# Folding the modulation weights on VectorE instead of multiplying them on TensorE, in a two-block transformer kernel

## The chip, the cores and the metric

The kernel runs on one core of one Trainium2 chip. The core has a matrix engine (TensorE, PE in the profile; its weight loads are PEld), a vector engine (VectorE, DVE), an activation engine (ScalarE, ACT), GpSimd (POOL) and a queue that issues most transfers (SyncE, SP). SBUF is the working memory, PSUM holds what TensorE writes. The metric is the time of one execution on the device in microseconds (us); lower is better.

## What is computed

Two blocks of two layers each on 256 tokens of width 1024, all in f32. The first block is a diffusion-style one: a vector `c` (for the latent tokens) and a vector `c_ctx` (for 256 context tokens) give, per layer, six modulation vectors of length 1024 each:

```python
for l in range(2):
    mod   = silu(c)     @ w_ada[l] + b_ada[l]          # w_ada[l]: 1024 x 6144
    mod_c = silu(c_ctx) @ w_ada[l] + b_ada[l]
    sh1, sc1, g1, sh2, sc2, g2 = split(mod, 6)         # the same for mod_c: csh1, ...
    h  = rms_norm(x,  norm1_g[l]) * (1 + sc1)  + sh1
    hc = rms_norm(xc, norm1_g[l]) * (1 + csc1) + csh1
    y, yc = mixer_sublayer(h, hc, ...)                 # qkv, Fourier mix, two attentions, gates, w_out
    x = x + g1 * y
    h = rms_norm(x, norm2_g[l]) * (1 + sc2) + sh2
    x = x + g2 * expert_choice_ffn(h, ...)             # 16 experts, each takes 32 tokens
    if l == 0:                                         # the same for the context tokens
        xc = xc + cg1 * yc
        xc = xc + cg2 * expert_choice_ffn(modulated rms_norm(xc), ...)
```

In layer 1 only the latent tokens go on, so `c_ctx` counts there for sh1 and sc1 alone. The second block (three kinds of attention and a cross attention to a memory, two layers) is not touched.

## The kernel before

All large weights stream through `ring`, four slots of 2 MB in SBUF. `slab_plan` (L53) writes down the order of all slabs; SP issues them in that order (L597 to L603), and slab i waits until slab i-4 has been used. TensorE tells that in order, with `last_release` (L717: a drain of the engine, then an increment of `slab_used`).

A layer of the first block has a **mixer** and an **experts** stage. In the mixer TensorE does three slabs of qkv products (`qkv_group`, four token tiles t each), three slabs of gates (`gate_group`, b = 0 to 2, four column groups j each), the attention (`pairs_pe`), one slab of branch products, three slabs of gates (b = 3 to 5) and one more of branches. VectorE copies odd qkv tiles out of PSUM, takes the sums of squares of the q and k heads (L2123 and L2124), waits for ScalarE's root of them (`rstd`, L1975), scales the heads and rotates them (L2133 to L2138, L2064 to L2069), then serves the attention (`pairs_dve`) and multiplies and adds the gated branches (L2162 to L2170). TensorE transposes the rotated heads in `turn_heads` (L843), the first of them behind gate group (1, 2).

The experts stage starts with two w_out slabs (L973), the second norm, the router logits (L991) and the choice of tokens, a chain of small steps on VectorE that ends with `slots` (L2262) and `select` (L2269). TensorE then gathers the chosen tokens (L1024), and goes through 16 experts: four slabs of gate and up weights (L1159), transposes (L1181) and two slabs of down weights (L1194). Between its waits it is kept busy with throwaway matmuls (`keep_warm`, L722).

The 24 slabs of `w_ada` (12 a layer, 512 columns each; slab n is called ada n) are handled in three steps. `ada_product` (L697) multiplies a slab by both vectors on TensorE, 32 matmuls of which each has a 128x32 operand `CT` (two columns of it are the two vectors, the rest is zero) and 128 columns of weights; four of them write to four groups of 32 partitions. ScalarE copies the result (`ada_row`, L1544), TensorE transposes it (`ada_turn`, L711), and ScalarE adds the bias into `MODT` (`ada_column`, L1551). Ada 0 to 3 are done at the very start. Ada 4 to 17 are spread over the mixer of layer 0, a product behind every second group and its transpose behind the next. Ada 18 to 21 lie at the start of the experts of layer 0 (18 behind the first tile's transpose, 19 and 20 between the gathers, 21 ahead of expert 0, its transpose behind expert 0's gate and up products and ahead of `scaled_rows`, L1048). Ada 22 and 23 lie at the start of the experts of layer 1. Their slabs stand in the plan at the same places: ahead of the slab that follows them in the mixer, and behind the two w_out slabs for 18 to 23.

Of the kernel before, what the change touches and what calls it, by code (L numbers as in the profile page):

```python
# [19 lines left out]
ALU = mybir.AluOpType  # L20
# [3 lines left out]
P = 128  # L24
# [10 lines left out]
RING = 4  # L35
# [10 lines left out]
ADA_LAST = 18  # L46
# [5 lines left out]
def slab_plan():  # L52

    plan = []
    for l in range(DEPTH):
        mixer = [("qkv", s) for s in range(3)] + [("gate", s) for s in range(3)] + [("branch", 0)]
        mixer += [("gate", 3 + s) for s in range(3)] + [("branch", 1)]
        for n, (kind, s) in enumerate(mixer):
# [14 lines left out]
    for l in range(DEPTH):  # L73
# [9 lines left out]
            {(0, 0): 4, (0, 1): 5, (1, 0): 0, (1, 1): 1}]  # L83

# [12 lines left out]
def shared_signals():  # L97
# [28 lines left out]
    ada_done=12, ada_mm=12, ada_row=12, ada_turned=12, mod=3, ld_dft=32, qk_turned=8, qkt=8, rope=4,  # L126
# [37 lines left out]
def build(nc, a, out, ctx):  # L164
# [40 lines left out]
    ct = sb("ct", KC * 32)  # L205
    modt = sb("modt", DEPTH * 96)
# [78 lines left out]
    CT = ct[:, :].rearrange("p (k n) -> p k n", k=KC)  # L285
    WR = wr[:, :].rearrange("p (l k e) -> p l k e", l=DEPTH, k=KC)
# [61 lines left out]
    slab_used = sem("slab_used")  # L348

# [321 lines left out]
    def _(pe):  # L671
# [9 lines left out]

        def ada_product(n, b=6, held=False):
# [6 lines left out]
            if n == 0:  # L689
                pe.wait_ge(*at("ct", 1))  # L690
            elif n >= ADA_LAST:
                pe.wait_ge(*at(f"ada_done@{l}", s))
            else:
                pe.wait_ge(*(at(f"ada_row@{l}", m) if m else at("ada_row@0", 12)))
            for k in range(KC):
                for j in range(4):
                    mm = pe.matmul(ps[b][32 * j:32 * j + 32, 0:P], CT[:, k, :],  # L697
                                   w[:, k, paired(j) if 6 <= s < 10 else slice(j * P, j * P + P)],
                                   start=(k == 0), stop=(k == KC - 1))
# [146 lines left out]
        def mixer(l):  # L846
# [37 lines left out]
            for s in (1, 2):  # L884
                for t in range(4):
                    qkv_group(l, s, t)
                    if l == 0:
                        step = 2 * (s - 1) + t // 2
                        if t % 2 == 0:
                            if s == 2:  # L890
                                ada_product(4 + t // 2)
                            fourier_tokens(0, step)
                        else:
                            if s == 2:
                                ada_turn(4 + t // 2)
# [6 lines left out]
            for b in range(3):  # L902
                for j in range(4):
                    gate_group(l, b, j, tokens)
                    if l == 0:
                        ada = 6 + 2 * b + j // 2
                        if j % 2 == 0:
                            ada_product(ada)
                        else:
# [1862 lines left out]
```

## Time and profile before

| what | us |
|---|---|
| median of 3 runs | 2285.1 |
| lowest and highest | 2284.4, 2285.84 |
| profiled execution, whole | 2280.98 |
| profiled execution, span of the core | 2279.1 |

| stage | us of the span | TensorE | transfers |
|---|---|---|---|
| start and mixer, layer 0 | 0 to 458 | nearly always busy | about half the time |
| experts, layer 0 | 458 to 1042 | busy | at their rate (415 to 424 GB/s) from about 600 on |
| mixer, layer 1 | 1042 to 1267 | busy | about a third |
| experts, layer 1 | 1267 to 1810 | waits for transfers | at their rate from 1328 on |
| second block | 1810 to 2279 | busy | about a quarter |

A row of the timeline gives start and duration in us, engine, line, operation, output and inputs by their names, shapes, and in brackets the idle time ahead of it with what ended it. "issue" stands for idle time that no other engine's work explains. A row can merge several instructions (x64). An f32 matmul is two instructions in these counts. Differences of two starts are the time from one piece of work to the next, which is less than a duration where instructions overlap.

### The profile page before, as it was taken

The page shows a single profiled execution, that of the slowest core. Times are in us where ns is not written, and L with a number is a line of the kernel's source. Part 1 is how long each engine was busy: PE and PEld are TensorE (multiplying, and loading weights), DVE is VectorE, ACT ScalarE, POOL GpSimd, SP SyncE. Part 2 cuts the span into 40 slices and gives each one's busy share as a digit, 9 for nine tenths or more (in the row PEclk, how much of TensorE's full clock was granted, in tenths as well). Part 3 has the DMA queues.
Part 4 walks back from the last instruction along what each step waited for, and adds up shares of the span by engine and source line. Part 5 has one row for each costly group of instructions (what it writes and reads, how often), then busy time and mean ns, then how long its engine had stood idle before and what let it go on. Part 6 is the DMA issues. An engine that isn't in the chain of part 4 may idle for free.

```text
span 2279.1 us, 31723 instructions
## 1 busy us (share of the span) xinstructions
PE 1986.8 (87%) x13681; PEld 1093.5 (48%) x13681; DVE 623.2 (27%) x1483; ACT 435.3 (19%) x1095; POOL 26.9 (1%) x52
## 2 busy tenths in 40 slices
PE   7999999999988898889999975667776699999997
PEld 4445554456434444334768641233432347564765
DVE  2012640135112221223351321201101235333533
ACT  2122621013111111002161110100000122222222
POOL 3000000000000000000000000000000000000000
PEclk9999999999999999999999997889989999999999
DMA  9544244227899999994314589999999933233320
GB/s 290 185 160 173 75 142 171 94 74 272 349 424 421 423 422 422 420 419 170 129 57 185 217 353 424 423 416 415 418 415 419 364 111 111 87 135 111 111 83 19
DMA packets 133832, 576.03 MB, mean 253 GB/s; under 512 B 7448, under 2 KB 16128, under 8 KB 92736
## 3 DMA queue, kind: packets, MB, share of 16 engines
q1 hardware_dynamic: 129312, 556.82, 61.8%
q0 software_dynamic: 3872, 17.00, 2.2%
q8 instruction: 110, 1.80, 0.3%
q10 hardware_dynamic: 512, 0.19, 0.0%
q14 instruction: 26, 0.21, 0.0%
HBM read 572.93 MB, written 1.05 MB: 252 GB/s over the span
## 4 chain that ended last, share of the span: by engine, by line
PE 53%; DMA 19%; issue 10%; PEld 8%; DVE 5%; PEldq 2%; ACT 2%; SPq 0%; POOL 0%; DVEq 0%; POOLq 0%
DMA ring<-w_up_e 14%; PE ps L788 8%; PE ps L1159 6%; PE ps L1250 5%; PE ps L973 4%; PE ps L1258 3%; PEld ps L1194 3%; PE ps L804 2%; PE ps L1392 2%; PE ps L777 2%; PEldq L717 2%; DMA ring<-w_xkv 2%; DMA ring<-w_down_e 2%; PE ps L1226 1%; PE ps L1229 1%
## 5 line engine op out<-in xcount | busy, mean ns | idle before, releaser
L1159 PE MATMUL ps<-ring,reg_bc 128*32 128x512 f32 x2960 | 382.4, 653 | 125.9 <-DMA ring<-w_up_e 118.1
L1159 PEld LDWEIGHTS ps<-ring,reg_bc 128*32 128x32 f32 x2960 | 91.9, 115 | 393.7 <-DMA ring<-w_up_e 199.8
L788 PE MATMUL ps<-reg_a,ring 128*128 128x512 f32 (+1 forms) x768 | 253.9, 488 | 5.5 <-issue 4.4
L788 PEld LDWEIGHTS ps<-reg_a,ring 128*128 128x128 f32 x768 | 143.5, 190 | 104.6 <-issue 92.7
L2352 DVE TENSOR_TENSOR xall<-xall,ps 128x512 f32<-128x512 f32 x48 | 32.8, 687 | 446.0 <-PE ps L1125 446.0
L1250 PE MATMUL ps<-ring,reg_a 128*128 128x512 f32 (+2 forms) x448 | 142.7, 474 | 2.6 <-issue 2.3
L1760 ACT ACTIVATE reg_bc<-ps 128x512 f32<-128x512 f32 x48 | 28.7, 597 | 562.4 <-PE ps L1159 562.4
L2395 DVE TENSOR_TENSOR reg_a<-ps,reg_e 32x256 f32<-32x256 f32 x192 | 80.7, 420 | 199.8 <-PE ps L1194 197.4
L1194 PE MATMUL ps<-ring,reg_bc 128*32 128x256 f32 x2048 | 117.8, 380 | 16.2 <-issue 14.7
L777 PE MATMUL ps<-ring,reg_a 128*128 128x512 f32 (+1 forms) x288 | 112.8, 546 | 1.9 <-issue 1.5
L1250 PEld LDWEIGHTS ps<-ring,reg_a 128*128 128x128 f32 x448 | 74.0, 190 | 65.1 <-issue 63.7
L1194 PEld LDWEIGHTS ps<-ring,reg_bc 128*32 128x32 f32 x2048 | 70.3, 110 | 54.7 <-issue 21.1
L1194 PE MATMUL ps<-ring,reg_e 128*32 128x256 f32 x1024 | 67.2, 406 | 31.4 <-issue 17.6
L1258 PE MATMUL ps<-reg_a,ring 128*128 128x256 f32 x384 | 88.9, 390 | 6.1 <-ACT reg_d L1798 5.0
L804 PE MATMUL ps<-reg_d,ring 128*128 128x512 f32 (+1 forms) x256 | 84.2, 488 | 1.7 <-issue 0.8
L973 PE MATMUL ps<-ring,reg_bc 128*128 128x512 f32 x192 | 84.2, 594 | 0.6 <-issue 0.5
L1258 PEld LDWEIGHTS ps<-reg_a,ring 128*128 128x128 f32 x384 | 74.0, 196 | 17.0 <-issue 7.0
L777 PEld LDWEIGHTS ps<-ring,reg_a 128*128 128x128 f32 x288 | 54.2, 190 | 56.2 <-issue 54.5
L804 PEld LDWEIGHTS ps<-reg_d,ring 128*128 128x128 f32 x256 | 48.1, 190 | 35.6 <-issue 30.4
L1568 ACT ACTIVATE reg_e<-ps 128x512 f32<-128x512 f32 (+1 forms) x48 | 23.6, 491 | 207.9 <-PE ps L788 207.8
L1194 PEld LDWEIGHTS ps<-ring,reg_e 128*32 128x32 f32 x1024 | 34.5, 116 | 57.1 <-issue 29.2
L1705 ACT ACTIVATE reg_bc<-ps,modt,scl 128x128 f32<-128x128 f32 x96 | 36.2, 458 | 129.2 <-PE ps L1024 129.2
(356 smaller groups left out, 2161.5 us busy)
## 6 DMA issues: line engine op xcount, KB each, us to landing
ring<-w_down_e SPq DMA_DIRECT2D x64, 2048.0 KB, 14.9
ring<-w_gate_e SPq DMA_DIRECT2D x123, 1024.0 KB, 10.6
ring<-w_up_e SPq DMA_DIRECT2D x123, 1024.0 KB, 13.6
ring<-w_in SPq DMA_DIRECT2D x34, 2048.0 KB, 8.1
ring<-w_ada SPq DMA_DIRECT2D x24, 2048.0 KB, 8.2
ring<-w_out SPq DMA_DIRECT2D x8, 2048.0 KB, 7.9
ring<-w_xkv SPq DMA_DIRECT2D x8, 1024.0 KB, 14.1
ring<-w_br_global SPq DMA_DIRECT2D x4, 1024.0 KB, 6.4
```

The costliest lines, as they stand in the source:

```text
L717: pe.drain().then_inc(slab_used, 1)
L777: mm = pe.matmul(ps[t][:, c0:COL], HT[:, k, t * P:t * P + P], w[:, k, c0:COL], start=(k == 0), stop=(k == KC - 1))
L788: mm = pe.matmul(ps[j][:, 0:n], w[:, k, j * P:(j + 1) * P], HT[:, k, 0:n], start=(k == 0), stop=(k == KC - 1))
L804: mm = pe.matmul(ps[n % 4][:, 0:tokens], w[:, k, j * P:(j + 1) * P], OT[:, k, 0:tokens], start=(k == k0), stop=(k == k1 - 1))
L973: mm = pe.matmul(ps[b][:, :], MT[:, k, t * P:t * P + P], w[:, k, :], start=(k == 0), stop=(k == KC - 1))
L1159: mm = pe.matmul(ps[s][32 * j:32 * j + 32, :], XGT[l][:, e // 4, s, 2 * q + k, e % 4 * CAP:(e % 4 + 1) * CAP], w[j // 2][:, k, (j % 2) * C ...
L1194: mm = pe.matmul(ps[4 + s][32 * j:32 * j + 32, 0:SEQ], HE[l][:, s, k, q * CAP:(q + 1) * CAP], w[:, k, j * SEQ:(j + 1) * SEQ], start=(q == ...
L1250: fill(name, lambda b: [pe.matmul(ps[b][:, 0:c1 - c0], src[:, k, t * P:t * P + P], w[:, k, c0:c1], start=(k == 0), stop=(k == KC - 1)) for ...
L1258: fill(name, lambda b: [pe.matmul(ps[b][:, 0:SEQ], w[:, k, c * P:(c + 1) * P], src[:, k, :], start=(k == 0), stop=(k == KC - 1)) for k in ...
L1392: yield pe.matmul(ps[b][:, :], OT2[:, k, t * P:t * P + P], w[:, k, :], start=(q == 0), stop=(q == KC - 1))
L1705: ins = act.activation(XGT[l][:, g, s, k, :], ps[6 + h][:, kk * P:(kk + 1) * P], ACT.Identity, scale=SCL[:, l, 1, k, s:s + 1], bias=MODT[: ...
L2395: ins = dve.tensor_tensor(OE[l][r:r + CAP, e // 4 % 2, s, j * SEQ:(j + 1) * SEQ], ps[4 + s][CAP * j:CAP * (j + 1), 0:SEQ], GB[CAP * j:CAP ...
```

## The change

The slabs ada 4 to 23 no longer go through TensorE whole. VectorE folds each of them (`fold`): for each of the 8 rows k that a partition holds it multiplies the 512 weights by that row's element of the vector, and adds it to a running sum. For ada 4 to 15 that is done for both vectors, in 16 instructions (2 of `tensor_scalar`, 14 of `scalar_tensor_tensor`). From ada 16 on only the latent tokens' vector is used; the even and the odd rows have a sum each, in 8 instructions (2 and 6). An instruction waits for the one before the last (semaphore `fold`), which writes the sum that it reads. TensorE (`ada_sum`) adds the two sums over the partitions: 8 matmuls, with `pick` (ones in one column, zeros in the others) as the 128x32 operand. A slab is given back by VectorE (`ada_folded`), so SP waits for VectorE at 20 places of its order.

The places move too. Ada 4 to 19 are all in the mixer of layer 0, ada 20 to 23 in the mixer of layer 1, by the table `ADA_STEPS` on TensorE and ScalarE, and each slab stands in the plan behind the mixer's slab. Nothing of them is left in the experts stages. On VectorE the folds stand at fixed places: 4 to 7 ahead of its four qkv copies, 8 and 9 between the sums of squares and the wait for the root, 10 to 12 ahead of the attention, 13 to 19 (in layer 1: 20 to 23) between the two halves of the branch merges.

```diff
@@ slab_plan
-            if l == 0 and 2 <= n < 9:
-                plan += [("ada",) + divmod(ada, 12) for ada in (2 * n, 2 * n + 1)]
-            plan.append((kind, l, s))
+            early = [("ada",) + divmod(ada, 12) for ada in ADA_BEHIND[l].get(n, ())]
+            plan += [(kind, l, s)] + early
         plan += [("out", l, s) for s in range(2)]
-        plan += [("ada", 1, s) for s in ((6, 7, 8, 9), (10, 11))[l]]
@@ sync
-                sp.wait_ge(slab_used, i - RING + 1)
+                sp.wait_ge(*slab_freed(i - RING))
@@ tensor
+        def ada_sum(n, b=6):
+            l, s = divmod(n, 12)
+            pe.wait_ge(*at(f"ada_folded@{l}", s + 1 - (0 if l else ADA_FOLDED)))
+            pe.wait_ge(*(at(f"ada_row@{l}", s) if s else at("ada_row@0", 12)))
+            for v in range(2):
+                chosen = 0 if n >= ADA_ALONE else v
+                for j in range(4):
+                    mm = pe.matmul(ps[b][32 * j:32 * j + 32, 0:P], pick[:, 32 * chosen:32 * chosen + 32],
+                                   folded(n)[:, v, paired(j) if 6 <= s < 10 else slice(j * P, j * P + P)],
+                                   start=(v == 0), stop=(v == 1))
+            mm.then_inc(sem(f"ada_mm@{l}"), 1)
@@ tensor, experts
             turn_tile(0)
-            if l == 0:
-                pe.wait_ge(*at("rexp@0", 1))
-            first = (18, 22)[l]
-            ada_product(first, 2)
+            keep_warm((6, 2)[l], 12)
             logits(0)
@@ vector
+        def fold(n):
+            ...
+            slab_wait(dve, i)
+            if n >= ADA_FOLDED + 2:
+                m = n - 2
+                dve.wait_ge(*(at(f"ada_mm@{m // 12}", m % 12 + 1)))
+            turns = [(k, v, k) for k in range(KC) for v in range(2)] if n < ADA_ALONE else [(k // 2, k % 2, k) for k in range(KC)]
+            for turn, v, k in turns:
+                c = CT[:, k, 0:1] if n >= ADA_ALONE else CT[:, k, v:v + 1]
+                if turn == 0:
+                    ins = dve.tensor_scalar(sums[:, v, :], w[:, k, :], c, None, ALU.mult)
+                else:
+                    dve.wait_ge(*at("fold", folds[0] - 1))
+                    ins = dve.scalar_tensor_tensor(sums[:, v, :], w[:, k, :], c, sums[:, v, :], ALU.mult, ALU.add)
+                ...
@@ vector, mixer
             dve.sem_inc(sem(f"qn@{l}_total"), 1)
+            if l == 0:
+                fold(8)
+                fold(9)
             rstd(f"qn@{l}", 40, HD)
+            if l == 0:
+                for n in (10, 11, 12):
+                    fold(n)
             pairs_dve(dve, link, f"at@{l}", pairs_block1(l))
             for half in range(2):
+                if half:
+                    for n in (range(13, 20), range(20, 24))[l]:
+                        fold(n)
+                    modulation(l, 1)
```

VectorE in the mixer of layer 0, before: from the last sums of squares to the scaling of the heads (`st` holds the sums and roots, `norm_rs` is ScalarE's root).

```order
L2123 TENSOR_TENSOR reg_d<-reg_bc 128x640 [waits dve_step]
L2124 TENSOR_REDUCE st<-reg_d 128x10 [waits dve_step]
L1973 TENSOR_SCALAR st<-st 128x40 [waits dve_step]
L1975 TENSOR_TENSOR st<-st 128x40 [waits norm_rs,dve_step]
L1976 TENSOR_TENSOR st<-st 128x40 [waits dve_step]
```

The same place after the change (`ada_mm` is TensorE's sum of an earlier slab, `ring` the weights, `ct` the vectors).

```order
L2151 TENSOR_TENSOR reg_d<-reg_bc 128x640 [waits dve_step]
L2152 TENSOR_REDUCE st<-reg_d 128x10 [waits dve_step]
L2060 TENSOR_SCALAR reg_d<-ring,ct 128x512 [waits dve_step,ada_mm,slab_landed0]
L2060 TENSOR_SCALAR reg_d<-ring,ct 128x512
L2063 SCALAR_TENSOR_TENSOR reg_d<-ring,ct,reg_d 128x512 [waits fold] x14
L2060 TENSOR_SCALAR reg_e<-ring,ct 128x512 [waits ada_mm,slab_landed1]
L2060 TENSOR_SCALAR reg_e<-ring,ct 128x512
L2063 SCALAR_TENSOR_TENSOR reg_e<-ring,ct,reg_e 128x512 [waits fold] x14
L1973 TENSOR_SCALAR st<-st 128x40
L1975 TENSOR_TENSOR st<-st 128x40 [waits norm_rs,dve_step]
```

Thirty-two instructions on slabs ada 8 and 9 now stand ahead of the wait for the root.

TensorE at the end of the choice of tokens in layer 0, before (L1024 gathers, L697 are products on a slab, L1006 turns the slots, L1159 is expert 0).

```order
L1024 MATMUL ps<-tmp,reg_d 128x128 [waits sel_first]
L1024 MATMUL ps<-tmp,reg_d 128x128 x7
L697 MATMUL ps<-ring,ct 32x128 [waits ada_done,slab_landed1]
L697 MATMUL ps<-ring,ct 32x128 x31
L1006 MATMUL ps<-ident,reg_e 128x16 [waits slots]
...
L1024 MATMUL ps<-tmp,reg_d 128x128 [waits xgt,sel_first]
L1024 MATMUL ps<-tmp,reg_d 128x128 x7
L697 MATMUL ps<-ring,ct 32x128 [waits ada_done,slab_landed2]
L697 MATMUL ps<-ring,ct 32x128 x31
L1159 MATMUL ps<-ring,reg_bc 32x512 [waits xgt,slab_landed3]
```

The same place after the change.

```order
L1055 MATMUL ps<-tmp,reg_d 128x128 [waits sel_first]
L1055 MATMUL ps<-tmp,reg_d 128x128 x7
L1037 MATMUL ps<-ident,reg_e 128x16 [waits slots]
L1037 MATMUL ps<-ident,reg_e 128x16
L1055 MATMUL ps<-tmp,reg_d 128x128 [waits xgt,sel_first]
L1055 MATMUL ps<-tmp,reg_d 128x128 x7
...
L1178 MATMUL ps<-ring,reg_bc 32x512 [waits xgt,slab_landed1]
```

The products on ada 20 and 21 are gone from between the gather and the slots, and from ahead of expert 0.

## Rows read from the trace of the kernel before

**Rows 1.** The page's second part: transfers in 40 equal slices, tenths busy.

```profile
DMA  9544244227899999994314589999999933233320
```

**Rows 2.** Timeline of TensorE in mixer 0: first and last product, and what follows.

```profile
103.18 1.96 PE L697 MATMUL ps<-ring,ct 128*32 128x128 f32 x64
105.42 1.96 PE L820 MATMUL ps<-tmp,reg_bc 128*128 128x512 f32 x4 [0.29 <-issue]
...
392.64 1.95 PE L697 MATMUL ps<-ring,ct 128*32 128x128 f32 x64
394.89 7.11 PE L788 MATMUL ps<-reg_a,ring 128*128 128x512 f32 x16 [0.29 <-issue]
```

**Rows 3.** Timeline of VectorE: 512 columns, without and with a wait between.

```profile
172.17 0.69 DVE L2137 TENSOR_TENSOR reg_bc<-reg_bc,gains 128x512 f32<-128x512 f32 x1
172.78 0.28 DVE L2138 TENSOR_TENSOR reg_bc<-reg_bc,gains 128x128 f32<-128x128 f32 x1
...
242.01 0.88 DVE L586 TENSOR_SCALAR reg_bc<-reg_bc,st 128x512 f32<-128x512 f32 x2
...
317.78 0.69 DVE L2165 TENSOR_TENSOR tmp<-ps,reg_e 128x512 f32<-128x512 f32 x1 [2.74 <-PE ps L804]
318.51 0.69 DVE L2168 TENSOR_TENSOR reg_bc<-reg_bc,tmp 128x512 f32<-128x512 f32 x1
```

**Rows 4.** Groups by line and shape on VectorE: count, busy us, mean ns, idle.

```profile
L2526 DVE SCALAR_TENSOR_TENSOR reg_bc<-reg_bc,st 128x256 f32<-128x256 f32 x8 | 3.5, 479 | 0.0
L2168 DVE TENSOR_TENSOR reg_bc<-reg_bc,tmp 128x256 f32<-128x256 f32 x8 | 3.4, 426 | 0.3
```

**Rows 5.** Timelines of VectorE and TensorE around the root of the heads, mixer 0.

```profile
141.40 0.19 DVE L1973 TENSOR_SCALAR st<-st 128x40 f32<-128x40 f32 x1
170.39 0.20 DVE L1975 TENSOR_TENSOR st<-st 128x40 f32<-128x40 f32 x1 [28.80 <-ACT st L441]
...
187.29 0.28 DVE L2138 TENSOR_TENSOR reg_bc<-reg_bc,gains 128x128 f32<-128x128 f32 x1
...
166.97 0.27 PE L711 MATMUL ps<-ident,diag 128*128 128x128 f32 x1
...
190.99 2.04 PE L697 MATMUL ps<-ring,ct 128*32 128x128 f32 x64
```

**Rows 6.** Who waited for whom: us in total, times, longest.

```profile
DVE reg_bc L2162 <- PE ps L804: 148.3, 10, 95.2
```

**Rows 7.** The page's sixth part: a w_ada slab, KB and us to landing.

```profile
ring<-w_ada SPq DMA_DIRECT2D x24, 2048.0 KB, 8.2
```

**Rows 8.** Busy time by window; the last three columns are clock, DMA share, GB/s.

```profile
596.00:606.00 10.00, 8.70 (x76) 3.12 (x69) 0.91 (x3) 1.97 (x4) 0.00 (x0) 1.00 0.51 192
...
1322.00:1332.00 10.00, 9.63 (x78) 5.08 (x77) 0.00 (x0) 3.02 (x8) 0.00 (x0) 0.95 0.33 108
```

**Rows 9.** Timeline of TensorE from the first gathers to expert 0's second half.

```profile
547.39 0.29 PE L1006 MATMUL ps<-ident,reg_e 16*128 16x16 f32 x2 [1.54 <-DVE reg_e L2262]
...
548.50 5.37 PE L1024 MATMUL ps<-tmp,reg_d 128*128 128x128 f32 x32 [0.55 <-DVE tmp L2269]
553.79 2.04 PE L697 MATMUL ps<-ring,ct 128*32 128x128 f32 x64
556.13 7.38 PE L1159 MATMUL ps<-ring,reg_bc 128*32 128x512 f32 x64 [0.30 <-issue]
...
571.44 0.30 PE L711 MATMUL ps<-ident,diag 128*128 128x128 f32 x1 [0.29 <-issue]
572.55 3.90 PE L1048 MATMUL ps<-ident,modt 128*128 128x128 f32 x32 [0.81 <-ACT modt L1551]
...
583.34 2.12 PE L1024 MATMUL ps<-tmp,reg_d 128*128 128x128 f32 x16 [0.25 <-issue]
```

**Rows 10.** Timeline of TensorE: the slots' turn in layer 1.

```profile
1319.68 0.39 PE L1006 MATMUL ps<-ident,reg_e 16*128 16x16 f32 x2 [2.81 <-DVE reg_e L2262]
```

**Rows 11.** Windows at the gather of layer 0, columns as in rows 8.

```profile
548.00:551.00 3.00, 2.50 (x11) 2.50 (x12) 2.32 (x6) 0.70 (x4) 0.00 (x0) 0.51 0.94 377
```

More of the change, by code:

```diff
@@ L83, with released_by_vector @@
             {(0, 0): 4, (0, 1): 5, (1, 0): 0, (1, 1): 1}]
+def released_by_vector(p):
+    return p[0] == "ada" and 12 * p[1] + p[2] >= ADA_FOLDED
 def out_banks(l):
@@ L285, in build, with folded @@
     CT = ct[:, :].rearrange("p (k n) -> p k n", k=KC)
+    def folded(n):
+        if n < 13:
+            at0 = reg_e[:, 4096:5120] if n < 10 and n % 2 else reg_d[:, 2048:3072] if n % 2 else reg_d[:, 1024:2048]
+        elif n < 20:
+            at0 = reg_bc[:, 8192 + n % 2 * 1024:9216 + n % 2 * 1024]
+        else:
+            at0 = (reg_bc[:, 10240:11264], tmp[:, 1024:2048])[n % 2]
+        return at0.rearrange("p (v n) -> p v n", v=2)
     WR = wr[:, :].rearrange("p (l k e) -> p l k e", l=DEPTH, k=KC)
@@ L348, in build, with slab_freed @@
     slab_used = sem("slab_used")
+    def slab_freed(i):
+        if released_by_vector(plan[i]):
+            n = 12 * plan[i][1] + plan[i][2]
+            return at(f"ada_folded@{n // 12}", n + 1 - max(ADA_FOLDED, n // 12 * 12))
+        return slab_used, sum(not released_by_vector(p) for p in plan[:i + 1])
     def tile_order(l):
@@ L680, in turn_biases, with ada_step @@
             pe.transpose(ps[0][:, 0:P], vec0[:, :], ident[:, :]).then_inc(sem("vec_turned"), 1)
+        def ada_sum(n, b=6):
[9 more added lines that the diff above has]
+            mm.then_inc(sem(f"ada_mm@{l}"), 1)
+        def ada_step(l, place):
+            turn, product = ADA_STEPS[l].get(place, (None, None))
+            if turn is not None:
+                ada_turn(turn)
+            if product is not None:
+                ada_sum(product)
         def ada_product(n, b=6, held=False):
@@ L904, in mixer @@
                     gate_group(l, b, j, tokens)
-                    if l == 0:
[L906 to L909, printed above, removed]
-                            ada_turn(ada)
+                    ada_step(l, (b, j))
                     for m in heads_at(l, b, j):
@@ L1553, in ada_column, with ada_step @@
             ins.then_inc(sem(f"ada_done@{l}"), 1)
+        def ada_step(l, place):
+            turn, product = ADA_STEPS[l].get(place, (None, None))
+            if turn is not None:
+                ada_column(turn)
+            if product is not None:
+                ada_row(product)
         def fourier_middle(l, n):
@@ L1661, in mixer @@
                     gate_in(l, 3 + b, j, tokens)
[L1662 to L1665 removed]
+                    ada_step(l, (3 + b, j))
         def experts(l):
@@ L1726, in experts @@
             square(0)
+            act.wait_ge(*at(f"mod@{l}", 3 - l))
             modulated_tile(0)
             square(1)
-            first = (18, 22)[l]
-            ada_row(first, 2)
             modulated_tile(1)
-            ada_column(first, 2)
             exps(0)
@@ L1962, in _ @@
     def _(dve):
-        steps = [0]
+        steps, folds = [0], [0]
         def link(ins):
@@ L2044, in ada_column @@
             dve.tensor_tensor(MODT[:, 0, 4 * s:4 * s + 4, :], got, bias, ALU.add).then_inc(sem("ada_done@0"), 1)
+        def fold(n):
+            l, s = divmod(n, 12)
+            i = where[("ada", l, s)]
+            w = slab_view(i)
+            sums = folded(n)
+            slab_wait(dve, i)
[7 more added lines that the diff above has]
+                    ins = dve.tensor_scalar(sums[:, v, :], w[:, k, :], c, None, ALU.mult)
+                else:
+                    dve.wait_ge(*at("fold", folds[0] - 1))
+                    ins = dve.scalar_tensor_tensor(sums[:, v, :], w[:, k, :], c, sums[:, v, :], ALU.mult, ALU.add)
+                if (turn, v, k) == turns[-1]:
+                    ins.then_inc(sem(f"ada_folded@{l}"), 1)
+                else:
+                    ins.then_inc(sem("fold"), 1)
+                    folds[0] += 1
         def bias_columns():
@@ L2103, in mixer @@
             for s in (1, 2):
+                if l == 0:
+                    fold(2 + 2 * s)
                 qkv_in(l, s, 1)
+                if l == 0:
+                    fold(3 + 2 * s)
                 qkv_in(l, s, 3)
```

88 lines of the change are left out of this document (21 added, 67 removed), and 5 rows, old and new, of the table ADA_STEPS.

## Prediction

> **What bounds the kernel now.** I read the page's slices first, then the timeline of TensorE, the waits of VectorE, and the windows. The slices [rows 1] show transfers at their rate in the experts stages (the runs of 9) and far below it in the mixers and in the second block. In the mixers TensorE is the bound: in its timeline each piece starts where the last ends, products on w_ada among them [rows 2]. VectorE has room there: it waits 28.8 us for the root of the heads and is through with their scaling at 187.6 [rows 5], ahead of the attention, and waits up to 95.2 us between the two halves of the merges [rows 6]. At the start of the experts the choice of tokens on VectorE holds TensorE for a few us [rows 9, 10]. Behind it the stage's end is set by TensorE up to the point from which transfers never pause again, and by the transfers from there.
>
> So three things have to be priced: what TensorE is spared in the mixers, whether the folds are done when TensorE asks, and what the experts stages gain.
>
> **Term 1, TensorE in mixer 0.** Fourteen products (ada 4 to 17) go. The first takes 105.42 - 103.18 = 2.24 us, the last 394.89 - 392.64 = 2.25, drain of 0.29 included [rows 2]; over the fourteen the starts sum to 31.3. Sixteen sums come. A product is 64 instructions in 1.95 us [rows 2], a sum is 16 of the same shape, so 0.49 each, 7.8 together. It has no drain behind it. Its upper bound would be that plus 0.29 of issue, as behind a product, 12.5 together; I take 7.8, since a transpose, also behind a wait but without a drain, shows no such gap. Two more transposes cost some 0.1 each, and small waits for weights save as much. Term 1 is 31.3 - 7.8 = **-23.5 us**. Nothing covers TensorE there, so it all counts.
>
> **Term 2, do the folds keep up.** No row shows `scalar_tensor_tensor` over 512 columns. On 256 it takes 479 ns where `tensor_tensor` takes 426 [rows 4], so 0.05 more; `tensor_tensor` over 512 takes 0.69 and the next starts 0.61 after it [rows 3], or 0.73 where it waits for it [rows 3]. The fold waits only for the one before the last, which has ended by then, so I take 0.66 a step and keep 0.61 and 0.79 as ends. `tensor_scalar` over 512 is two in 0.88 [rows 3], some 0.42 each. A fold is 14 x 0.66 + 2 x 0.42 = 10.1 us (9.4 to 11.9), and 6 x 0.66 + 0.84 = 4.8 from ada 16 on. In all that is 12 x 10.1 + 8 x 4.8 = 160 us of VectorE, all in gaps, if each is in time. I went through the places in order, with 8.2 us from issue to landing [rows 7] and term 1's shift where it applies:
> - Folds 4 to 7 have 4 us or more to spare.
> - Fold 8 starts when ada 8 has landed, at 139.8: the slot is given back ahead of the four groups (7.1 each) and two products before 166.97 [rows 5], at 134.0, less 2.4 of shift, plus 8.2. The sums of squares before it end at 141.6 [rows 5] less 3 of shift. Folds 8 and 9 end at 139.8 + 20.2 = 160.0. TensorE is through with gate group (0, 3) at 166.97 [rows 5] less four products (9.2) plus five sums (2.5) = 160.3. So 0.3 to spare.
> - Behind it stands the sum of ada 9, its copy on ScalarE, and only then the root: some 3.6 us behind 160.3. VectorE then needs 187.6 - 170.4 = 17.2 [rows 5], to 181.2. TensorE asks for the rotated heads at 190.99 [rows 5] less 11.5 plus 2.9 = 182.4. So 1.2 to spare, where it had 5.4.
> - Folds 10 to 12 run from 181.2 to 211.5; the sum of ada 12 is asked for at 214.7.
> - Folds 13 to 19 need 3 x 10.1 + 4 x 4.8 = 49.5 us in the gap of 95.2 [rows 6], but wait for slots: ada 16 and 18 come when a gate slab is through on TensorE, land 8.2 later and are folded in 4.8, 13 us, against two gate groups (14.2): 1.2 to 1.6 to spare.
> - In mixer 1 the tightest is ada 23, 2 us.
>
> The same slots feed gate and branch slabs. SP's order has VectorE's releases in it now; the latest of these slabs lands 6 us ahead of need. Six margins of 0.3 to 3 us, each read to about 1: I take **+1 us** of stalls. At 0.61 a step it is 0. At 0.79 a fold is 11.9, and going down the same list 3.3 are lost at ada 9, 2.1 at ada 12 and 0.3 at ada 15: 5.7.
>
> The profile shows a vector instruction starting 0.61 after one that lasts 0.69 [rows 3], so neighbours overlap by 0.08. The Trainium skill ("VectorE: DVE Perf Modes", section "The DRAIN you can't avoid") says that the next one does not start until the pipe is empty; each step would then cost its whole 0.75 and a fold 11.3, with some 2.5 us of stalls for my 1. By the row the trace does not agree, and I stay with the row.
>
> **Term 3, experts of layer 0.** The products on ada 18 to 20 lie beside VectorE's chain to `slots`, for which TensorE waits anyway (1.54 idle) [rows 9]; taking them away moves nothing. Ada 21 is on the path: 556.13 - 553.79 = 2.3 [rows 9]. Its transpose and the wait for its column, 572.55 - 571.44 = 1.1 [rows 9], too. Term 3 is **-3.4 us**.
>
> The six slabs that leave these stages (2 MB, 5.0 us each at the 422 GB/s of the full slices; 30 us) are the larger promise. But transfers still have a pause later: in 596 to 606 they are half busy [rows 8], as all four slots are full and TensorE is on the weights of expert 1 that came by another way. What is loaded earlier before that is lost in the pause, and TensorE's position at 600 sets the rest. In layer 1 the pause is at 1322 to 1332, 0.33 busy [rows 8], right before expert 0 frees its first slot. So I price the moved loads at 0. If the pauses were gone they would bring up to 30.
>
> **Term 4, layer 1.** Four sums (2.0) and four transposes (0.4) are new in mixer 1: **+2.4 us**. Ada 22 and 23 lie in the shadow of the chain to `slots` (2.81 idle in spite of them [rows 10]): -0.2 for a transpose behind the throwaway matmuls.
>
> **Term 5, TensorE's clock.** With ada 19 and 20 gone TensorE idles for 1.54 [rows 9] plus two products, 5.7 us, ahead of the slots in layer 0, and in layer 1 for 2.81 [rows 10] plus ada 23's product, transpose and wait (3.4), 6.2. In 548 to 551, behind the short gap of today, the granted clock is 0.51 [rows 11], the lower of its two levels (1.2 of 2.4 GHz), and 32 instructions of gathers take 5.37 [rows 9], where 16 take 2.12 at full clock [rows 9]. All at the lower level they would take 8.5: 3.1 more. So 0 to 3.1 in layer 0 and about as much, with expert 0's first products, in layer 1. The clock is down today already, so most of the price is being paid; I take 0.5 each, **+1 us**.
>
> The Trainium skill ("TensorE: Matmul & The Clock Gate", section "What's actually happening") has the throttled clock as the default that activity releases. By it the longer gap alone would put all the gathers at 1.2 GHz, which is the rival below.
>
> **Sum.** -23.5 + 1 - 3.4 + 2.4 - 0.2 + 1 = -22.7 us. The second block is only moved. Against the profiled execution, 2280.98, that is 2258.3; the median of the runs lies 4.1 above it, so 2285.1 - 22.7 = **2262.4 us**. With the ends of the sum's price (+4.7, and 1.2 in mixer 1), no stalls or clock loss (-2) and 2 us for all that was read to a tenth here, this forecast's own range is 2258 to 2269.
>
> **Rivals.**
> - *The folds run at the waiting pace*, 0.79 a step or more, because the waits between them show. For it: a neighbour that waits starts after 0.73 [rows 3]. Against: the fold waits for the one before the last. Stalls 5.7 for 1: 2267.
> - *The clock falls in the two gaps* and stays down through gathers and expert 0's start. 6.2 for 1: 2268.
> - *The moved loads count after all*: the experts' transfers start 30 us ahead. Against: both pauses [rows 8]. 2262 - 30 = 2232.
> - *VectorE becomes the bound of mixer 0, slower than before.* If a step took 1.05, a fold would be 15.5. By the list above the stalls are 2 x 15.5 - 20.5 at ada 9, 3 x 15.5 - 33.6 at ada 12, 3 x 15.5 - 35.4 at ada 15, together 34.5, and 7 at ada 7: 2285.1 - 23.7 + 41.5 = 2303. It decides against the change from a step of about 0.92 on. Against: nothing on VectorE with 512 columns of f32 and one result takes over 0.69 [rows 3], and 0.05 is what this form adds [rows 4].
>
> **How the numbers follow.** Forecast 0.72, slow folds 0.1, clock 0.08, loads count 0.05, slower 0.05. The first three reach from 2258 to 2269; with the slab landings and the spread of term 1 I give 2255 to 2271, which leaves out the last two. About 0.2%, 4.6 us, is what can be told from no change. Faster: 0.72 + 0.1 + 0.08 + 0.05 = 0.95, less 0.02 for cases between; same 0.02; slower 0.05.
>
> **What would show it.** In the new profile: a fold instruction every 0.66 us; TensorE's sums taking 0.5; the heads' scaling on VectorE ending near 181, the experts stage of layer 0 beginning near 436 (458 less 22.5), expert 0 at 531.9 (556.1 less 22.5, less 2.3, plus 0.5); the pause of transfers still there near 576 and 1300; mixer 1 longer by 2.4. Idle time of TensorE ahead of the sum of ada 9 or of the heads' transposes would show term 2 wrong, a gather of 8 us term 5, and a shift that grows inside the experts stages the pricing of the loads at 0.

## Result and profile after

| what | before | changed |
|---|---|---|
| median, us | 2284.75 (4 runs) | 2263.96 (4 runs, 2262.29 to 2266.87) |
| ratio, 95% interval | | 0.9912 (0.9895 to 0.9929) |
| profiled execution, whole / span | 2280.98 / 2279.1 | 2266.87 / 2265.0 |

The forecast was 2262.4 (2255 to 2271). By the medians 20.8 us are gained, by the two profiled executions only 14.1: before was profiled in one of its shortest executions, the changed kernel in its longest. So both kernels were profiled once more (below), and the stages are compared over two profiles each. They are read from the starts of TensorE's pieces; the last row ends with TensorE's last piece, some 8 us before the span does:

| from ... to, us | before | again | changed | again | forecast |
|---|---|---|---|---|---|
| start to w_out, layer 0 | 458.3 | 458.8 | 435.9 | 434.3 | -22.5 |
| of it, ahead of the first qkv group | 63.0 | 63.2 | 61.8 | 60.5 | 0 |
| of it, behind | 395.3 | 395.6 | 374.1 | 373.9 | -22.5 |
| w_out to expert 0 | 97.8 | 100.2 | 97.7 | 97.8 | -2.9 |
| expert 0 to mixer 1 | 487.1 | 490.5 | 487.4 | 488.3 | 0 |
| mixer 1 to w_out, layer 1 | 223.7 | 223.7 | 228.6 | 227.2 | +2.4 |
| w_out to expert 0, layer 1 | 59.0 | 59.2 | 61.8 | 59.2 | +0.3 |
| expert 0 to second block | 487.2 | 487.4 | 487.3 | 486.9 | 0 |
| second block | 458.2 | 458.3 | 458.5 | 458.5 | 0 |

From start to w_out the means differ by -23.4 (-2.0 and -21.4 in its two parts), from w_out on by -1.3, -0.9, +4.2, +1.4, -0.2 and +0.2, -20.0 in all. The gain is made in mixer 0 and partly given back in mixer 1.

The 2.0 us ahead of the first qkv group cannot be counted to the change. They arise between 20 and 29 us, at TensorE's second product on w_ada and the pieces behind it, which are in both kernels. Here is that product, in the first profile of before and in the second of the changed kernel:

```profile
20.12 3.64 PE L697 MATMUL ps<-ring,ct 128*32 128x128 f32 x64 [0.94 <-DMA ring<-w_ada]
```

```profile
20.11 1.95 PE L744 MATMUL ps<-ring,ct 128*32 128x128 f32 x64 [1.21 <-DMA ring<-w_ada]
```

It takes 3.64 in both profiles of before, 3.35 and 1.95 in those of the changed kernel, and 3.64 again in experiments 4 and 7, which are changed kernels too and reach the qkv groups at 62.9 and 63.0.

**The folds.** Timeline of VectorE, changed kernel, folds of ada 8 and 9 and the root of the heads (answers to rows 3 to 5). Columns: start, duration, engine, line, operation, output and inputs, shapes, count, idle time ahead.

```profile
140.59 0.88 DVE L2060 TENSOR_SCALAR reg_d<-ring,ct 128x512 f32<-128x512 f32 x2 [2.92 <-DMA ring<-w_ada]
141.38 9.36 DVE L2063 SCALAR_TENSOR_TENSOR reg_d<-ring,ct,reg_d 128x512 f32<-128x512 f32 x14
150.66 0.88 DVE L2060 TENSOR_SCALAR reg_e<-ring,ct 128x512 f32<-128x512 f32 x2
151.45 9.36 DVE L2063 SCALAR_TENSOR_TENSOR reg_e<-ring,ct,reg_e 128x512 f32<-128x512 f32 x14
...
180.79 0.28 DVE L2169 TENSOR_TENSOR reg_bc<-reg_bc,gains 128x128 f32<-128x128 f32 x1
181.00 0.87 DVE L2060 TENSOR_SCALAR reg_d<-ring,ct 128x512 f32<-128x512 f32 x2
```

A fold starts 150.66 - 140.59 = 10.07 us after the last (forecast 10.1). One `scalar_tensor_tensor` lasts 0.745; fourteen in a row take 9.36, so the step, from one start to the next, is (9.36 - 0.745) / 13 = 0.663 (forecast 0.66). The slab of ada 8 lands at 140.6 (forecast 139.8), fold 9 ends at 160.8 (160.0), the scaling at 181.07 (181.2).

Timeline of TensorE, the same place and the first rotated heads (answers to rows 5):

```profile
159.97 0.27 PE L757 MATMUL ps<-ident,diag 128*128 128x128 f32 x1
160.86 0.66 PE L721 MATMUL ps<-reg_e,pick 128*32 128x128 f32 x16 [0.62 <-DVE reg_e L2063]
161.82 0.67 PE L834 MATMUL ps<-reg_a,ring 128*128 128x512 f32 x1 [0.29 <-issue]
...
182.61 0.60 PE L889 MATMUL ps<-ident,reg_bc 128*128 128x128 f32 x4
```

TensorE asks for the sum of ada 9 at 160.2, waits 0.62, and finds the heads ready at 182.6. This is its only wait for a fold. Its sums last 0.64 to 0.67, not 0.49.

**The experts.** The busy time of the engines by window; the last three columns are the granted clock (the share of full speed that TensorE is granted), the share of transfers and GB/s (answers to rows 8):

```profile
568.00:578.00 10.00, 9.90 (x96) 3.38 (x92) 0.00 (x0) 0.00 (x0) 0.00 (x0) 1.00 0.51 188
...
1298.00:1308.00 10.00, 4.56 (x25) 3.89 (x24) 7.23 (x24) 0.00 (x0) 0.00 (x0) 0.75 0.06 25
...
1307.50:1317.50 10.00, 9.63 (x73) 5.10 (x71) 0.00 (x0) 3.01 (x8) 0.00 (x0) 0.88 0.31 108
```

The pauses of transfers are still there. In layer 0 they are half busy near 573 as near 600 before. In layer 1 the window of [rows 8] begins 3.9 us ahead of expert 0; the window at the same distance now has 0.31 for 0.33, and ahead of it, at 1298 to 1308, they are nearly idle (0.06). So the slabs that no longer load in the experts made the pauses longer: between w_out and mixer 1 the share of transfers is 0.86 where it was 0.90, over the same 585 us, which is some 23 us more of idle time for four slabs of 5.0. The timeline of TensorE at the slots of layer 0 (answers to rows 9):

```profile
526.90 0.39 PE L1037 MATMUL ps<-ident,reg_e 16*128 16x16 f32 x2 [5.81 <-DVE reg_e L2298]
528.10 5.57 PE L1055 MATMUL ps<-tmp,reg_d 128*128 128x128 f32 x32 [0.81 <-DVE tmp L2305]
533.61 2.78 PE L1178 MATMUL ps<-ring,reg_bc 128*32 128x512 f32 x24
```

The idle time is 5.81 (forecast 5.7), the gathers take 5.57 (5.37 before), and expert 0 follows without ada 21's product. It starts at 533.6, 1.7 later than forecast, and the loss lies ahead of these rows:

```profile
483.12 3.72 PE L1022 MATMUL ps<-wr,reg_a 128*128 128x16 f32 x32 [0.26 <-issue]
486.69 3.28 PE L1004 MATMUL ps<-ring,reg_bc 128*128 128x512 f32 x4
...
486.00:490.00 4.00, 4.00 (x14) 1.94 (x14) 0.55 (x3) 0.62 (x4) 0.00 (x0) 0.65 0.89 369
```

Four products of w_out take 3.28 us where such four take 1.96 at full clock [rows 2]; the window says that the granted clock fell, behind 32 router products of 16 columns, with TensorE busy throughout. The forecast knew of no fall here.

### The profile page after: what moved, and what is told of

Its sections match the earlier page's. It is cut to its first block, busy times and chain, and to the rows that moved or that the text cites. A ratio compares the mean times of both kernels' runs of the same rounds, so it can differ in the third digit from the quotient of the medians.

```text
span 2265.0 us, 30108 instructions
## 1 busy us (share of the span) xinstructions
PE 1969.0 (87%) x12745; PEld 1076.5 (48%) x12745; DVE 782.7 (35%) x1742; ACT 433.6 (19%) x1095; POOL 26.8 (1%) x52
## 4 chain that ended last, share of the span: by engine, by line
PE 54%; DMA 20%; issue 8%; PEld 7%; DVE 6%; PEldq 3%; ACT 2%; SPq 0%; POOL 0%; DVEq 0%; ACTq 0%; POOLq 0%
DMA ring<-w_up_e 15%; PE ps L834 10%; PE ps L1178 5%; PE ps L1268 5%; PE ps L1004 4%; PE ps L850 4%; PE ps L1276 3%; PEld ps L1212 3%; DMA ring<-w_down_e 3%; PE ps L1410 2%; PE ps L823 2%; PEldq L763 2%; PEld ps L1055 1%; DMA ring<-w_xkv 1%; PE ps L1247 1%
## 5 line engine op out<-in xcount | busy, mean ns | idle before, releaser
L2412 DVE TENSOR_TENSOR reg_bc<-reg_bc,ps 128x256 f32<-128x256 f32 x48 | 20.1, 419 | 138.1 <-ACT reg_bc L1771 138.1
```

## Experiments

**1. Placement alone.** The kernel before, with ada 18 to 23 as products in the mixers.

```diff
-            if l == 0 and 2 <= n < 9:
+            if l == 0 and 2 <= n < 10:
                 plan += [("ada",) + divmod(ada, 12) for ada in (2 * n, 2 * n + 1)]
+            if l == 1 and n in (8, 9):
+                plan += [("ada",) + divmod(ada, 12) for ada in (2 * n + 4, 2 * n + 5)]
...
-        plan += [("ada", 1, s) for s in ((6, 7, 8, 9), (10, 11))[l]]
...
-                    if l == 0 and b < 2 and j % 2 == 0:
-                        ada_product(14 + 2 * b + j // 2)
-                    elif l == 0 and b < 2:
-                        ada_turn(14 + 2 * b + j // 2)
+                    ada = (14, 18)[l] + 2 * b + j // 2
+                    if l == 0 or b:
+                        (ada_product if j % 2 == 0 else ada_turn)(ada)
```

> The kernel before with the placement alone changed: slabs ada 18 to 23 are taken out of the experts stages and multiplied on TensorE in the mixers (18 and 19 in the last gate slab of mixer 0, 20 to 23 in the last two of mixer 1), nothing is folded. If slabs moved out of the experts are worth nothing, as the prediction has it, the time is that of before, 2284.8, plus six products of 2.25 in the mixers (13.5) and their transposes (0.6), less 3.4 in the experts of layer 0 and 0.2 in layer 1, plus 2.7 for the lower clock that the changed kernel shows ahead of the slots of layer 1: 2298 us (2294 to 2301). If the 30 us of transfers count, it is 2268.

Measured: 2305.4 (2305.05 to 2308.43), ratio 1.0091 (1.0077 to 1.0106). 20 us slower, and slower than the 2294 to 2301 expected. The 12 MB that no longer load in the experts bring nothing that shows: from w_out to mixer 1 it takes 588.3 us, where before has 584.9 and 590.7, and the 30 us of the rival are not there. The mixers pay more than expected, 5.7 and 16.5 for two and four products. One reason stands in TensorE's timeline of mixer 1:

```profile
1256.10 6.43 PE L787 MATMUL ps<-reg_a,ring 128*128 128x256 f32 x16 [3.79 <-DMA ring<-w_in]
1262.45 1.95 PE L696 MATMUL ps<-ring,ct 128*32 128x128 f32 x64
```

Two w_ada slabs stand ahead of the gate slab, whose transfer is issued at 1248.3, when the first product has given back its slot: TensorE waits 3.8 us for it, and the sixteen instructions behind take 6.43 where 3.7 is usual: from 1255 to 1261 the granted clock is 0.50. Each slab still adds work to the bound engine of the mixers; folding is what makes the new place affordable.

**2 and 3. How far to fold.** The changed kernel, with only ada 4 to 17 (or 4 to 18) folded, and the others multiplied in the experts where products stood before. Below is the core of the second. In the first, ADA_PRODUCTS is 18, the products at these places are 18, 19 and 20, and 21 stands ahead of expert 0.

```diff
+ADA_PRODUCTS = 19
...
-    return p[0] == "ada" and 12 * p[1] + p[2] >= ADA_FOLDED
+    return p[0] == "ada" and ADA_FOLDED <= 12 * p[1] + p[2] < ADA_PRODUCTS
...
-            keep_warm((6, 2)[l], 12)
+            if l == 0:
+                pe.wait_ge(*at("rexp@0", 1))
+            first = (19, 22)[l]
+            ada_product(first, 2)
             logits(0)
...
+                ada_product(20, 2)
                 gather(0, 1, 0)
+                ada_turn(20, 2)
                 gather(0, 1, 1)
+                ada_product(21, 2)
                 turn_slots(0)
+                ada_turn(21, 2)
```

> The changed kernel with the folding of ada 4 to 17 alone: 18 to 21 are products in the experts of layer 0 and 22, 23 in those of layer 1, where they stood before. Against the changed kernel, 2264.0, mixer 1 loses four sums and transposes (its first block of gates with sums there takes 3.65 us longer than in the kernel before), mixer 0 two of some 0.9 each, the stage ahead of layer 1's slots gets back the full clock (2.7 by the two traces), and the experts of layer 0 have the 3.4 again that term 3 took: 2264.0 - 3.65 - 1.8 - 2.7 + 3.4 = 2259.3. If the lower clock in layer 1 came by chance and not from the product that is gone, 2262. If the moved slabs had been worth something, it would be slower than the changed kernel, up to 2290.

> As the one that folds to 17, and ada 18 folded too, so that 19, 20 and 21 are the products beside VectorE's choice of layer 0's tokens, and none is left behind it. Term 3 (-3.4) should then be whole, for one sum and transpose of 0.9: 2.5 less than the one that folds to 17, 2256.8, and so some 7 below the changed kernel. If TensorE's wait for the slots does not hide three products, it is no faster than the other.

Measured: 2264.3 (2257.96 to 2268.02), ratio 0.9906 (0.9889 to 0.9922), and 2260.0 (2256.2 to 2265.58), ratio 0.9892 (0.9874 to 0.991). Both are slower than expected (2259.3 and 2256.8). Folding to 17 alone is as fast as the whole change. The next slab brings 4.3 for the 2.5 expected, but the intervals overlap. In the traces mixer 1 is back at 57.3 us between its two branches (60.8 to 60.9 with four sums), and the experts' front in layer 0 takes 102.0 and 98.9: the order is that of term 3. The size is uncertain: in both the clock is low for 6.8 us behind the router, and such falls move this stretch by 2 to 4 us.

**4. Throwaway products for the clock in layer 1.**

```diff
+        def spare_product(b):
+            for k in range(KC):
+                for j in range(4):
+                    pe.matmul(ps[b][32 * j:32 * j + 32, 0:P], CT[:, k, :], ident[:, :],
+                              start=(k == 0), stop=(k == KC - 1))
...
-            keep_warm((6, 2)[l], 12)
+            keep_warm(6, 12) if l == 0 else spare_product(2)
...
                 turn_affinities(0)
+                spare_product(2)
                 scaled_rows()
```

> The changed kernel, with throwaway products of the same 64 instructions on resident data in the two places of layer 1's experts where ada 22 and 23 were multiplied before (12 throwaway bf16 products make room for the first). If the clock that falls at 1283 to 1293 and 1303 to 1308 is what the missing products cost, the router's products of the second tile take 1.9 us instead of 3.4 and the gathers 4.7 instead of 5.8: 2264.0 - 2.7 = 2261.3. If it falls by chance, 2264.

Measured: 2263.8 (2263.1 to 2265.06), ratio 0.9908 (0.9892 to 0.9924). No gain. The front of layer 1's experts takes 59.2 us, but so it does in the changed kernel's second profile, without any spare product. So the 2.7 us that the first profile lost there are no fixed cost of the change. Over all profiles, this front takes 61.8 us in two of the six without a product there and at most 59.7 in the six with one: whether the missing product makes a fall likelier stays open.

**5. Folds at the waiting pace.** Both sums of a fold one after the other, each instruction waiting for the one just ahead.

```diff
-            turns = [(k, v, k) for k in range(KC) for v in range(2)] if n < ADA_ALONE else [(k // 2, k % 2, k) for k in range(KC)]
+            if n < ADA_ALONE:
+                turns = [(k, v, k) for v in range(2) for k in range(KC)]
+            else:
+                turns = [(k, v, 2 * k + v) for v in range(2) for k in range(KC // 2)]
...
-                    dve.wait_ge(*at("fold", folds[0] - 1))
+                    dve.wait_ge(*at("fold", folds[0]))
```

> The changed kernel with each fold's two sums built one after the other, so that every instruction waits for the one just ahead of it and not for the one before that. This is the pace of the rival 'the folds run at the waiting pace': 0.73 to 0.79 a step for the 0.663 measured, a fold of 11 to 12 us for 10.1. By the prediction's list of places the stalls at ada 9, 12 and 15 are then 3 to 5.7 us where they were about 1, so 2264.0 + 2 to 4.7 = 2266 to 2269. If the pace stays at 0.66, or the margins are larger than the list has them, 2264.

Measured: 2271.2 (2270.23 to 2273.2), ratio 0.9938 (0.9925 to 0.9952). Timelines of VectorE and TensorE at ada 9:

```profile
151.12 5.48 DVE L2066 SCALAR_TENSOR_TENSOR reg_e<-ring,ct,reg_e 128x512 f32<-128x512 f32 x7
156.51 0.48 DVE L2063 TENSOR_SCALAR reg_e<-ring,ct 128x512 f32<-128x512 f32 x1
157.03 5.48 DVE L2066 SCALAR_TENSOR_TENSOR reg_e<-ring,ct,reg_e 128x512 f32<-128x512 f32 x7
...
162.56 0.67 PE L721 MATMUL ps<-reg_e,pick 128*32 128x128 f32 x16 [2.75 <-DVE reg_e L2066]
```

The step is (5.48 - 0.75) / 6 = 0.79, a fold 11.8, as the rival had it. TensorE waits 2.75 at ada 9, 1.56 at ada 12, 0.19 at ada 15 (the list said 3.3, 2.1, 0.3), and 0.39 and 0.28 at ada 5 and 7, for which the list had nothing: 5.2 where it is 0.6. The median is 7.2 higher, where 2 to 4.7 were expected. The waits make 4.6 of it. In this profile the clock is low from 233.4 to 236.8 besides, which it is in neither profile of the changed kernel; how much of the other 2.6 that is, is not shown. The wait between neighbours is worth taking out.

**6. Longer folds.** The first instruction of each sum seven times, ada 4 to 15.

```diff
+                    for _ in range(6 if n < ADA_ALONE else 0):
+                        dve.tensor_scalar(sums[:, v, :], w[:, k, :], c, None, ALU.mult).then_inc(sem("fold"), 1)
+                        folds[0] += 1
+                        dve.wait_ge(*at("fold", folds[0]))
                     ins = dve.tensor_scalar(sums[:, v, :], w[:, k, :], c, None, ALU.mult)
```

> The changed kernel with the first instruction of each sum issued seven times in the folds of ada 4 to 15 (each waits for the one ahead; the value is the same), to make a fold longer by 12 tensor_scalar of about 0.5: 16.1 us for 10.1. This is the rival 'VectorE becomes the bound of mixer 0' made real. By the list: stalls of 2 x 16.1 - 20.5 = 11.7 at ada 9, 3 x 16.1 - 33.6 = 14.7 at ada 12, 3 x 16.1 - 35.4 = 12.9 at ada 15 and 7.6 at ada 7, together 46.9 for 1: 2310 us, slower than before by 25. If the folds' gaps hold more than the list says, it stays below 2290.

Measured: 2334.2 (2333.61 to 2337.35), ratio 1.0217 (1.0203 to 1.0231), 70 us over the changed kernel where 46 were expected. A fold is 16.3. TensorE's waits for folds, from the trace: 9.1 for ada 4 and 5, 8.4 for 6 and 7, 11.1 for 8 and 9, 10.6 for 11 and 12, 11.1 for 14 and 15, 50.4 in all. The list had 46.9, without ada 4 and 5; at its own places 41.3 were measured. Yet w_out starts 68.7 us later than in the changed kernel. The other 19 us stand behind the waits. TensorE and its windows at ada 9:

```profile
194.94 1.08 PE L721 MATMUL ps<-reg_e,pick 128*32 128x128 f32 x16 [8.50 <-DVE reg_e L2067]
196.30 4.61 PE L834 MATMUL ps<-reg_a,ring 128*128 128x512 f32 x5 [0.29 <-issue]
...
190.00:194.00 4.00, 0.00 (x0) 0.00 (x0) 4.00 (x7) 0.00 (x0) 0.00 (x0) 0.63 0.00 0
195.00:199.00 4.00, 3.71 (x20) 1.70 (x20) 0.56 (x3) 2.84 (x5) 0.00 (x0) 0.50 0.42 104
```

Over the first 480 us the granted clock is 0.94 in the mean (1.00 in the changed kernel's mixer 0). It falls during the wait and is at 0.50 behind it: the sum takes 1.08 for 0.66, five gate instructions 4.61 where five take 2.31 elsewhere. There are seven waits of 4.9 to 8.5 us. In the 10 us from the end of each, the granted clock is 0.75, 0.64, 0.68, 0.79, 0.75, 0.73 and 0.69: what is missing to 1 adds up to 19.7 us of full speed. So the 19 us are the clock's, 2.7 a wait. The short waits of experiment 5 bring no fall: its sum at ada 9, behind 2.75 us, takes 0.67.

**7. What a sum costs.** Every sum issued twice.

```diff
-            for v in range(2):
+            for v in (0, 1, 0, 1):
                 chosen = 0 if n >= ADA_ALONE else v
```

> The changed kernel with every one of the 20 sums issued twice in a row (the second starts anew, so the value is the same). In the trace of the changed kernel a sum with its transpose costs 0.91 us in mixer 1 (3.65 for four), where the prediction had 0.6. If that is the price of the 16 instructions, the second sums cost 20 x 0.6 to 0.7 = 12 to 14: 2277. If it comes from the change of operands ahead of the sum and behind it, a second sum in a row costs the bare 0.49, 9.8 together: 2273.8, and the pieces of gates behind a sum are as long as before.

Measured: 2273.2 (2270.69 to 2277.01), ratio 0.9948 (0.9935 to 0.9962), 9.2 over the changed kernel (8.0 over its later runs, below), 0.40 to 0.46 for each of 20. TensorE in mixer 1, of the changed kernel first, then with doubled sums:

```profile
1206.66 0.66 PE L721 MATMUL ps<-reg_bc,pick 128*32 128x128 f32 x16
1207.26 3.72 PE L834 MATMUL ps<-reg_a,ring 128*128 128x256 f32 x16
1210.81 0.27 PE L757 MATMUL ps<-ident,diag 128*128 128x128 f32 x1
1211.02 0.66 PE L721 MATMUL ps<-tmp,pick 128*32 128x128 f32 x16
```

```profile
1221.50 0.27 PE L757 MATMUL ps<-ident,diag 128*128 128x128 f32 x1
1221.71 1.12 PE L721 MATMUL ps<-tmp,pick 128*32 128x128 f32 x32
1222.76 3.72 PE L834 MATMUL ps<-reg_a,ring 128*128 128x256 f32 x16
```

Thirty-two instructions take 1.12 where sixteen take 0.66: the bare price is 0.46. The rest comes with the change from one kind of piece to another; what in it costs the time is not shown. From its start to the gate piece behind it a sum is 0.60, the transpose ahead of it takes a slot of 0.21, and the gate pieces between them last a little longer (1210.81 - 1207.26 = 3.55, where sixteen of an unbroken row of 64 in 14.05 take 3.5). Per sum and transpose mixer 1 pays (227.2 - 223.7) / 4 = 0.9 us (second profile), where 0.6 was forecast.

**8. The router's products apart.** The kernel that folds to 18, with large products between the two groups.

```diff
                 logits(2)
-                logits(3)
                 out_group(1, 0, 0, 2)
+                logits(3)
+                out_group(1, 0, 2, 4)
                 turn_affinities(1)
-                out_group(1, 0, 2, KC)
+                out_group(1, 0, 4, KC)
```

> The kernel that folds to 18, with the two groups of router products of layer 0 (16 instructions of 16 columns each) no longer in a row: four large products of w_out stand between them. In its profile the clock is at its lower level for 6.8 us from 2.7 us after the first of them on, and the stretch from w_out to the slots is 4.7 us longer than in the kernel before. If what lets the clock fall is TensorE's two groups of small products in a row, it stays up there and the kernel gains 3 to 4: 2260.0 - 3.5 = 2256.5. If the fall comes by chance or from what is ahead of the router, 2260.

Measured: 2257.2 (2254.23 to 2259.71, 6 runs), ratio 0.9882 (0.9864 to 0.9901). The clock stays up behind the router, and the front of layer 0's experts takes 95.7 us, the shortest of all profiles. But in this profile it is low for 6.8 us later, in the chain to the slots, and against the kernel that folds to 18 the ranges of runs overlap. So that the order holds the clock up is not shown. What is shown is that this kernel beats the changed one: on the same chip every one of its runs is below every run of the changed kernel (next), by 8 us in the medians, some 27 below before.

**9 and 10. The same kernels again.**

> The changed kernel again, nothing else: a second profile of the same instructions. The theory that the 1.9 us lost between the router of layer 0 and the slots, and the 1.6 at the router of layer 1, are falls of the clock that an execution has or has not, and no cost of the change, expects one of them to be gone or to be of another length, and the time to stay at 2264 (2261 to 2267). If they belong to the order of this kernel's instructions, they stand at the same places with the same length.

> The kernel before again, nothing else: a second profile. If falls of the clock behind the router's products of layer 0 come and go, this one may have one (w_out to the slots 91 to 93 us) where the first had none (89.1). If they are the change's, it has none again.

Measured: changed 2265.2 (2261.03 to 2269.47, 6 runs), ratio 0.9916 (0.9898 to 0.9935); before one run at 2287.8, beside 2284.4 of its 11 in that group. The stages are in the first table. The timeline of TensorE and a window, before, second profile, behind the router in layer 0:

```profile
505.94 3.72 PE L991 MATMUL ps<-wr,reg_a 128*128 128x16 f32 x32 [0.26 <-issue]
509.50 2.67 PE L973 MATMUL ps<-ring,reg_bc 128*128 128x512 f32 x4
...
508.00:512.00 4.00, 4.00 (x20) 2.30 (x20) 0.55 (x3) 0.62 (x4) 0.00 (x0) 0.83 1.05 400
```

The first profile of before has no fall there, the second has one, and its stretch from w_out to expert 0 is 2.4 us longer. In the changed kernel the fall behind the router of layer 0 is in both profiles. At the router of layer 1 the first profile has the clock low for 10.2 us, from 1285.9 on, the second for 3.4, from 1288.0 on. The windows, first profile and second:

```profile
1285.00:1290.00 5.00, 5.00 (x28) 4.39 (x29) 1.37 (x4) 1.51 (x4) 0.00 (x0) 0.59 0.29 116
```

```profile
1284.00:1289.00 5.00, 4.58 (x38) 3.80 (x37) 1.92 (x7) 2.34 (x9) 1.05 (x2) 0.90 0.07 28
```

So whether such a fall comes, and how long it lasts, can differ between two executions of one kernel. That a kernel's order makes it likelier is not excluded. The Trainium skill ("TensorE: Matmul & The Clock Gate", section "What's actually happening") calls the chip's look at activity free-running, not tied to the kernel's start; two profiles of one program that differ in their falls agree with that.

## Why the prediction held

- **Terms 1 and 2 (-22.5; measured -21.4 behind the start, over two profiles each).** That w_out began at 435.95 where 436 was written is in part luck: 1.2 us of it came ahead of the first qkv group. Two of the prices were off as well. Between the two branches of mixer 0 the kernel before takes 127.2 us with six products, the kernel that folds to 18 takes 117.0 with six sums, the changed one 117.9 with seven. So a sum with its transpose is worth 0.9 us (0.6 in the forecast) and a product with its own 0.9 + 10.2 / 6 = 2.6 (2.34 in the forecast): both left out what a change of operands costs the pieces beside them. 14 times 0.26 and 16 times 0.3 nearly cancel, which is luck too. The stalls were 0.3 to 0.6, not 1. With these sizes the sum is -36.4 + 14.4 + 0.5 = -21.5.
- **The rule on VectorE's pace.** By the sentence that the prediction quotes from the Trainium skill ("VectorE: DVE Perf Modes", section "The DRAIN you can't avoid") a step would have been 0.75 and a fold 11.3. The trace has 0.663 and 10.07. The prediction left out how the same paragraph goes on: a next instruction that is not held starts earlier. With that half the trace agrees, as each instruction starts 0.08 us before the one ahead has ended.
- **The places, one by one.** The step (0.663), the fold (10.07), its end at ada 9 (160.8 for 160.0), the end of the scaling (181.07 for 181.2) and the heads came out to 1 us. Experiment 5 made the list of margins visible: at 11.8 us a fold the waits fall at ada 9, 12 and 15 and are 0.1 to 0.6 shorter than listed. The list missed ada 5.
- **Rival "waiting pace".** Its condition did not hold. Where experiment 5 makes it hold, its step (0.79) and its waits (5.2 for 5.7) are as written, and the time is 2271 for 2267.
- **Rival "VectorE becomes the bound".** It did not come about, but its mechanism is real (experiment 6), and dearer than written, since waits of 5 us and more also bring the clock down. With that the change would probably lose from a step below the 0.92 written. The argument against it, that nothing on VectorE with 512 columns takes over 0.69, was too wide: two `reciprocal` of before take 3.35 each, and this form takes 0.745.
- **Term 3 (-3.4, less 0.5 for the clock; measured -1.3 in the front and -0.9 behind).** Products beside VectorE's chain cost nothing that shows: with three of them there experiment 8 has the shortest front, 95.7. That ada 21 was not free has the order of experiments 2 and 3 for it (102.0 with it ahead of expert 0, 98.9 without). How large it is cannot be told, since the clock moves this stretch by 2 to 4 us from execution to execution.
- **Moved loads at 0.** Right: experiment 1 has the loads moved and gains nothing of the 30 us, to within the 6 us by which the two profiles of before differ there (584.9 and 590.7), and the pauses of transfers stand where they stood and are longer.
- **Term 4 (+2.4; measured +3.5 in the second profile, +4.9 in the first).** The term that was mis-sized: 0.9 a sum with its transpose, not 0.6. The first profile has 1.3 us more in the attention besides, with a granted clock of 0.67 from 1134 to 1139.
- **Term 5 (+1).** In layer 0 the gathers lost 0.2 us (5.57 for 5.37), so the gap made less than the 0.5. In layer 1 they take 5.79 and 5.58 where before has 4.67 and 5.00, and the whole front is 2.6 us longer in one profile of two. So the rival "the clock falls in the two gaps" did not come about as priced: no gathers took 8 us.

The sum of the steps, -22.7, stands against -20.8 by the medians. By the first table mixer 0 falls short by 1.1 and mixer 1 by 1.8; the other stages lie within what the clock and the start move.

## What to carry over

Work moved from the bound engine to one with gaps pays where each gap is wide enough at the moment it is asked for: list the places with the hour at which each slab lands, each fold ends and each sum is asked for, and check the list at two paces. Do not move what already hides: here five of the six moved products ran in another engine's shadow, and the loads of all six were paid for by a pause. Leaving five slabs there, none of them ahead of expert 0, with the router's products apart, was faster than the whole change by 8 us; 3.6 of it is mixer 1 without its sums (57.3 for 60.9). Before a loss of 1 to 4 us in one profile is put down to a change, profile both kernels twice.

## What the runs showed of the hardware

- `scalar_tensor_tensor` over 128x512 f32 lasts 0.745 us; the next starts 0.663 after it if it waits for the one before the last (changed kernel), 0.79 if it waits for this one (experiment 5).
- TensorE's clock falls to the lower of its levels (0.50, 1.2 of 2.4 GHz) with no idle time shown over 0.3 us, behind 32 products of 16 columns (3.7 us), for 3.4 to 6.8 us, in 9 of the 11 profiles with these in a row.
- Behind waits of 4.9 to 8.5 us it is at that level too, which adds 2.7 us to each wait (experiment 6).
- A short group of small products between large ones costs more than its own pitch: 0.46 in a row (experiment 7), 0.60 between, and 0.9 with one transpose.
